# Sum of squares of x taken from its features instead of its rows, in the first stage of a two-layer hybrid block on one core

## What is computed

```python
def _rmsnorm(x, w=None):
    xf = x.astype(jnp.float32)
    y = xf * lax.rsqrt(jnp.mean(xf * xf, axis=-1, keepdims=True) + NORM_EPS)
    return y if w is None else y * w.astype(jnp.float32)

def _hybrid_layer(h, norm_w, w_in, ...):
    u = _rmsnorm(h, norm_w)
    proj = jnp.matmul(u, w_in.astype(jnp.float32))
    ...
    return jax.nn.sigmoid(gate_a) * y_a + jax.nn.sigmoid(gate_b) * y_b

# h = x;  h = h + hybrid_layer(h);  then rmsnorm and two more layers
```

## Time and profile before

| what | value |
|---|---|
| median of 3 runs (lowest, highest) | 2182.87 us (2181.63, 2183.14) |
| the profiled execution, its own time | 2180.54 us |
| its span in the trace | 2178.9 us |
| TensorE busy | 2151.7 us, 99% of the span |
| VectorE, ScalarE, GpSimd busy | 59%, 51%, 6% |
| mean DMA share, read from HBM | 58% of 16 engines, 389.94 MB |
| granted clock, mean | 0.998 |

### The profile page before, as it was taken

One profiled execution on the slowest core, in us unless ns is written; L12 is line 12 of the kernel. 1 busy time (PEld: TensorE's weight loads), 2 busy tenths in 40 slices (PEclk: granted clock), 3 DMA queues, 4 the chain that ended last, 5 costly groups with the idle time before them and its releaser, 6 DMA issues.

```text
span 2178.9 us, 32768 instructions
## 1 busy us (share of the span) xinstructions
PE 2151.7 (99%) x12468; PEld 1774.4 (81%) x12468; DVE 1279.1 (59%) x1505; ACT 1110.3 (51%) x1478; POOL 125.1 (6%) x204
## 2 busy tenths in 40 slices
PE   9999999999999999999999999999999999999998
PEld 7888888888888777787878888888888788888886
DVE  6455546454545758575765564466545845566466
ACT  6544545544444748374655554455444544445442
POOL 6000000000000100001010000000000110000001
PEclk9999999999999999999999999999999999999999
DMA  9766565565655544454546765745568566555654
GB/s 349 246 189 192 169 202 178 183 202 184 200 186 183 156 145 145 127 168 124 174 137 207 238 193 179 205 146 164 161 197 271 177 214 169 163 163 164 194 167 143
DMA packets 208610, 400.64 MB, mean 184 GB/s; under 512 B 13296, under 2 KB 30209, under 8 KB 208094
## 3 DMA queue, kind: packets, MB, share of 16 engines
q1 hardware_dynamic: 199824, 369.94, 53.8%
q0 software_dynamic: 6352, 20.49, 3.1%
q10 hardware_dynamic: 2304, 8.39, 1.1%
HBM read 389.94 MB, written 8.82 MB: 183 GB/s over the span
## 4 chain that ended last, share of the span: by engine, by line
PE 89%; ACT 3%; DVE 3%; issue 3%; DMA 1%; DVEq 0%; ACTq 0%; SPq 0%
PE stream_psum L611 27%; PE stream_psum L613 26%; PE stream_psum L612 26%; PE heads_psum L592 2%; ACT w_high L1049 1%; PE heads_psum L774 1%; DVE work L1631 1%; ACT work L1049 1%; DVE w_low L1468 1%; PE heads_psum L961 1%; PE heads_psum L923 1%; PE heads_psum L904 1%; DMA w_raw<-in_w_mem_kv 1%; PE heads_psum L793 1%; PE heads_psum L722 0%
## 5 line engine op out<-in xcount | busy, mean ns | idle before, releaser
L1468 DVE TENSOR_TENSOR w_low<-w_raw,w_high 128x1024 fp32r<-128x1024 f32 x688 | 831.1, 1225 | 636.2 <-ACT w_high L1049 634.9
L1049 ACT ACTIVATE w_high<-w_raw 128x1024 fp32r<-128x1024 f32 x688 | 712.8, 1058 | 455.3 <-PE stream_psum L613 386.4
L611 PE MATMUL stream_psum<-w_high,x_high 128*128 128x512 f32 x1856 | 741.9, 400 | 0.1
L613 PE MATMUL stream_psum<-w_high,x_low 128*128 128x512 f32 x1856 | 724.2, 390 | 0.9 <-issue 0.9
L612 PE MATMUL stream_psum<-w_low,x_high 128*128 128x512 f32 x1856 | 723.4, 390 | 0.0
L613 PEld LDWEIGHTS stream_psum<-w_high,x_low 128*128 128x128 f32 x1856 | 348.3, 188 | 75.6 <-issue 1.8
L611 PEld LDWEIGHTS stream_psum<-w_high,x_high 128*128 128x128 f32 x1856 | 348.7, 188 | 73.3 <-issue 2.5
L612 PEld LDWEIGHTS stream_psum<-w_low,x_high 128*128 128x128 f32 x1856 | 348.9, 188 | 69.1 <-issue 1.9
L611 PE MATMUL stream_psum<-w_high,y_high 128*128 128x512 f32 x896 | 353.3, 394 | 2.7 <-DVE y_low L1887 2.2
L613 PE MATMUL stream_psum<-w_high,y_low 128*128 128x512 f32 x896 | 349.7, 390 | 0.0
L612 PE MATMUL stream_psum<-w_low,y_high 128*128 128x512 f32 x896 | 349.5, 390 | 0.0
(11 more groups left out here) (295 smaller groups left out, 1214.9 us busy)
## 6 DMA issues: line engine op xcount, KB each, us to landing
w_raw<-in_w_in SPq DMA_DIRECT2D x528, 512.0 KB, 4.5
w_raw<-in_w_out SPq DMA_DIRECT2D x128, 512.0 KB, 5.0
w_raw<-in_w_mem_kv SPq DMA_DIRECT2D x32, 512.0 KB, 5.8
work<-rows_scratch POOLq DMA_DIRECT2D x8, 512.0 KB, 5.0
proj<-in_mem_t SPq DMA_DIRECT2D x8, 256.0 KB, 6.3
work<-in_x_t SPq DMA_DIRECT2D x4, 512.0 KB, 6.0
residual<-in_x SPq DMA_DIRECT2D x2, 1024.0 KB, 10.5
mkv_scratch<-proj POOLq DMA_DIRECT2D x4, 512.0 KB, 3.6
```

Source lines behind the costliest of these rows:

```text
L611: pe.matmul(acc, hi[:, k, sl(m)], w, start=first, stop=False)
L613: return pe.matmul(acc, lo[:, k, sl(m)], w, start=False, stop=final)
L1049: return act.activation(dst, src, func, **kw)
L1468: tt(WL[:, c % RING, :], RAW[:, c % RING, :], WH[:, c % RING, :].bitcast(F32), ALU.subtract).then_inc(lo_done, 1)
```

## The change

1. **x features** come in eight pieces of 256 KB (two 128-feature tiles each) instead of four of 512 KB, one behind each weight chunk of the second memory block. ScalarE and VectorE work on one piece a chunk, over all eight chunks, instead of two pieces a chunk over four.
2. **Sum of squares**: the two Squares of x rows with `accum_out` go. ScalarE squares the x features in `wk(0)` to `wk(3)` into `wk(4)` to `wk(7)` in two instructions of 2048 columns; GpSimd halves the 4096 columns four times with additions of 2048, 1024, 512 and 256 columns; TensorE multiplies the 256 that remain with a matrix of ones, in the side `gates` of `N_ML`; Ln and Exp read PSUM.
3. **Order**: on ScalarE the Squares now stand ahead of `narrow_high`, and both behind the second memory block's copy out of PSUM. Ln and Exp move into `gates`, whose steps on TensorE, ScalarE and VectorE are put off with longer gaps.
4. **x rows** (`RES`) come in four pieces of 512 KB in `N_GA` instead of two of 1 MB in the memory stage. `gated(0)` waits for them.

```diff
-        xt_in = [sem(f"x_features{c}_in") for c in range(4)]
+        xt_in = [sem(f"x_features{c}_in") for c in range(NCH)]
+        x_sums, x_ss = sem("x_square_sums"), sem("x_squares_summed")
...
-        X_AFTER = ((1, 4), (1, 6))
...
             def x_features(i):
-                sp.dma_start(wk(i, U).rearrange("p (c n) -> p c n", c=2), bass.AP(x_t.tensor, i * (4 * P * S), [[2 * S, P], [2 * P * S, 2], [1, 2 * S]])
-                             ).then_inc(xt_in[i], 16)
+                sp.dma_start(wk(i / 2, 2 * S), bass.AP(x_t.tensor, i * (2 * P * S), [[2 * S, P], [1, 2 * S]])).then_inc(xt_in[i], 16)
...
-                    if (half, c) in X_AFTER:
-                        m = X_AFTER.index((half, c))
-                        sp.dma_start(RES[:, m, :], x2[:, m, :]).then_inc(x_in[m], 16)
-                    if half == 1 and c < 4:
+                    if half == 1:
                         x_features(c)
...
-            group(N_GA, w_in, 0, IN1, [wide(C_GA + b * NBLK) for b in range(4)])
+            for b in range(4):
+                for c in range(NCH):
+                    put(N_GA, b * NCH + c, rows_in_chunk(w_in, C_GA + b * NBLK, IN1, c, [[1, NBLK]]))
+                    if b in (1, 2) and c % 4 == 0:
+                        m, half = b - 1, c // 4
+                        sp.dma_start(RES[:, m, sl(half, U)], x2[:, m, sl(half, U)]).then_inc(x_in[m], 16)
...
+                if b == 0:
+                    pool.wait_ge(norm_s, 2)
+                    for i, n in enumerate((2 * U, U, U // 2, U // 4)):
+                        if i:
+                            pool.wait_ge(x_sums, i)
+                        pool.tensor_tensor(wk(4, n), wk(4, n), wk(4 + n / U, n), ALU.add).then_inc(x_sums, 1)
...
-                yield from gap(9)
+                yield from gap(8)
+                pe.wait_ge(x_sums, 4)
+                for m in range(M):
+                    last = pe.matmul(H[:, 1, sl(m, 8)], wk(4, S)[:, sl(m)], ones[:, 0:8], start=True, stop=True)
+                last.then_inc(x_ss, 1)
+                yield from gap(12)
...
                 for c in range(NCH):
-                    act.wait_ge(xt_in[c // 2], 16)
+                    act.wait_ge(xt_in[c], 16)
                     for k in (2 * c, 2 * c + 1):
                         f(XH[:, k, :], wk(k / 4, S), ACT.Copy, scale=NC_[:, k:k + 1]).then_inc(x_hi, 1)
+                    yield from gap(2)
+                act.wait_ge(consts, N_CONSTS)
+                for i in range(2):
+                    f(wk(4 + 2 * i, D), wk(2 * i, D), ACT.Square).then_inc(norm_s, 1)
                     yield
                 narrow_high(0, GATE_W, GATE_RAW)
                 yield
-                for m in range(M):
-                    act.wait_ge(x_in[m], 16)
-                    f(wk(4, D), RES[:, m, :], ACT.Square, accum_out=ST[:, m:m + 1]).then_inc(norm_s, 1)
-                    act.wait_ge(norm_s, m + 1)
-                    yield from gap(2)
-                f(ST[:, 2:4], ST[:, 0:2], ACT.Ln, scale=1.0 / D, bias=eps_c).then_inc(norm_s, 1)
+
+            def gates():
+                yield from gap(10)
+                act.wait_ge(x_ss, 1)
+                f(ST[:, 2:4], H[:, 1, 0:16].rearrange("p (m n) -> p m n", m=M)[:, :, 0], ACT.Ln, scale=1.0 / D, bias=eps_c).then_inc(norm_s, 1)
                 act.wait_ge(norm_s, 3)
                 f(ST[:, 4:6], ST[:, 2:4], ACT.Exp, scale=-0.5).then_inc(norm_s, 1)
-
-            def gates():
+                act.wait_ge(norm_s, 4)
+                yield from gap(2)
...
@@ DVE x_prep @@
-                    yield
+                    yield from gap(2)
                 narrow_low(0, GATE_W, GATE_RAW)
...
@@ DVE gates @@
+                yield from gap(11)
...
@@ DVE gated @@
+                    if not base:
+                        dve.wait_ge(x_in[m], 32)
```

More of the change, by code:

```diff
@@ L1358, in _ @@
             small_block(0, 48, G_ACT, wk(11, S)[0:96, :])
-            act.wait_ge(norm_s, 4)
             mkv = [[(mkv_out[b], 16)] for b in range(2)]
```

## The result

| | before | with the change |
|---|---|---|
| median of 5 runs (lowest, highest) | 2183.14 us (2181.63, 2185.22) | 2193.54 us (2193.38, 2196.36) |
| the profiled execution (its span) | 2180.54 us (2178.9) | 2196.36 us (2194.7) |
| TensorE busy | 2151.7 us, 99% | 2156.3 us, 98% |
| granted clock, mean | 0.998 | 0.993 |

The ratio is 1.0051 (95% interval 1.0041 to 1.0062): slower by 0.5%, 10.4 us between the medians, where 11.8 were forecast. The two profiled executions lie at opposite ends of their runs, before's under its lowest of these five and the other at its highest, so their spans differ by more, 15.8 us. What belongs to the change has to be read stage by stage.

What follows compares the result with a forecast made beforehand. TensorE was taken as the bound, busy 2151.7 of 2178.9 us. Terms 10.0 - 0.24 + 1.7 + 0.35 = +11.8 us, on the median 2182.87, gave 2194.7 us, range 2189.5 to 2197.5.

Steps and rivals of the forecast that it cites:

- start of the small block: TensorE's small block after the memory stage, waiting for narrow_low, starts at 64.75 instead of 54.74: +10.0 us.
- the edge behind it, and the clock: From small block to N_ML: wait for ScalarE's PSUM copy gone, -0.24 us; half clock behind the gap, +1.7 us.
- product of ones and the rest: Two small matmuls added to TensorE's stream in N_ML: +0.35 us (bounds 0.2 and 0.6).
- sum for the stage: All terms added, 10.0 - 0.24 + 1.7 + 0.35: +11.8 us.
- Queue order: ScalarE runs block copy, two Squares, then narrow_high, so the small block waits; alone its start moves to 60.7, +5.95 us.
- Standstill: VectorE's narrow_low waits out GpSimd's 2048-column addition of 4.9 us, moving the small block's start from 60.7 to 64.75.
- rival 2: No standstill: narrow_low isn't held up by GpSimd's addition, small block at 60.7, sum +7.8, 2190.6 us; chance 0.12.
- The clock: TensorE's 10.6 us idle before the small block halves its clock for 3.4 us of work: +1.7 us (bounds 0, 3.4).
- rival 3: More than forecast: low clock lasts twice as long (+1.7), or the gates' chain stalls chunks; 2196 to 2199 us; chance 0.10.
- The product of ones: Two small matmuls in TensorE's N_ML stream, 0.36 us between their start and the stream's next: +0.35 us.
- The covers: Margins in gates (least 0.9 us), last feature piece and x rows in N_GA: no new TensorE wait, 0 us.

Runs made afterwards that it cites:

- run 1: The changed kernel with narrow_high put ahead of the two Squares on ScalarE, both still behind the block copy: 2186.93 us, ratio 1.0009.
- run 2: The changed kernel with GpSimd's additions made to wait for narrow_low too: 2191.34 us, ratio 1.0030.
- run 3: The changed kernel with GpSimd's additions cut into instructions of at most 512 columns: 2190.95 us, ratio 1.0033.
- run 5: The changed kernel with 48 unread identity matmuls on TensorE ahead of the small block, filling its gap: 2184.33 us, ratio 1.0004.
- run 8: Run 7 with the x rows back in the memory stage as two pieces of 1 MB, those in N_GA removed: 2192.35 us, ratio 1.0038.
- run 6: The changed kernel with narrow_high and narrow_low moved into the second memory block, behind the seventh piece of x features: 2184.97 us, ratio 1.0003.
- run 7: The changed kernel with both the early split of run 6 and the 512-column additions of run 3: 2188.70 us, ratio 1.0019.
- run 9: The changed kernel with Squares of 512 columns behind each feature piece, 512-column additions between GpSimd's stores, and run 6's early split: 2187.05 us, ratio 1.0013.
- run 10: The kernel before the change with 24 identity matmuls added between the memory stage and the small block: 2180.25 us, ratio 0.9984.
- run 11: The kernel before the change with 24 small matmuls of 32x8 added right behind the warm-up ones: 2174.52 us, ratio 0.9956.

## Why the prediction was right

The time, 2193.54, lies 1.2 us from the forecast 2194.7 and inside 2189.5 to 2197.5. Step by step, by the sum's own terms:

| term | forecast | measured | by |
|---|---|---|---|
| start of the small block | +10.0 | +9.8 | 64.55 less 54.74 |
| the edge behind it, and the clock | -0.24 + 1.7 | +2.5 | 71.04 - 64.55 less 58.71 - 54.74 |
| product of ones and the rest | +0.35 | +0.4 | what is left to 12.75 |
| sum for the stage | +11.8 | +12.75 | block copies |

- **Queue order**: right. The memory blocks' end, forecast at 54.15, lets the block copy start at 54.38, with 0.2 us of a later start in it. Run 1 leaves the split behind the block copy and still takes 9.1 us away: the two Squares ahead of it (3.6), the standstill that they bring with them (3.7), and with the shorter gap 1.5 of the clock. The 5.95 of the forecast is another thing, the whole delay of the start without the standstill; run 2, which is that case, starts the small block at 60.45, +5.7.
- **Standstill**: right, rival 2 is out. Run 2 takes 4.1 us away, and run 3 shows that its length follows that of the addition. I took 4.9 us for the addition of 2048 columns, from the slope between 512 and 1024; it took 4.50. The rows weren't of one kind: both are multiplications, and the one of 1024 columns reads a mask over and over (L502). An addition of 1024 columns in run 2 takes 2.38 us instead of the 2.482 of the earlier trace rows. The Trainium skill, page "GPSIMD Engine Reference", section "Elementwise — side-by-side cycle accounting", gives 4497 ns: the trace agrees, with 4496. The rule of the Trainium skill, page "SBUF — State Buffer", section "Who interferes with whom", which I had assumed over 2048 columns, holds here: `narrow_low` took 4.63 us.
- **The clock**: right in kind, and **the term that was mis-sized**. "Half of 3.4 us: +1.7" was taken from one recovery at the start. Here the half clock lasted through 5.9 us of work, and run 5 prices it at 2.7 us, 1.0 more than the term. That lies inside its bounds (0 and 3.4), nearer to rival 3's "twice as long" than to my value. One recovery was no measure of the next.
- **The product of ones**: 0.37 us to the stream's next start (83.82 to 84.19), as in the rows I took it from, but the next start comes 0.31 behind that instead of 0.23: 0.45 in all, where I counted 0.35.
- **The covers**: right. No new wait in `gates`, for the last piece of features, or in `N_GA`; the wait for `w_low` at 51 is gone, and run 8 shows what can make it.
- **The close agreement is partly luck.** From the median before, 2183.14 + 12.75 would be 2195.9. The 2.3 us between that and 2193.54 come from the scatter of the executions and from the delta stage, which one profile of each doesn't measure: before's was 2.6 us under its median, the other 2.8 over. The forecast had no term for the delta stage at all; its "issue" waits, the largest group of TensorE's waits in the profile before, were passed over as no wait for another engine.

What stays open: why one place of the delta stage's instructions is better than another, whether other counts do more, and what of the +2.5 us there is the change's own and what is scatter; runs 1 to 3 and 6 to 9 have between +0.2 and +3.1 there, from TensorE programs of the same length. No other counts than 24 and 48 were tried.

## What to carry to other kernels

Taking work off a busy engine is worth nothing if the new work stands ahead of something small that the bounding engine needs next: look at what the moved instructions are queued in front of, on each in-order queue, and put the small producer (`narrow_high`, `narrow_low`) first or well ahead. A VectorE instruction with two SBUF inputs waits for the end of a GpSimd addition that began before it (3.7 us here, of 4.50); cutting the GpSimd work into pieces shortens VectorE's waits but starves GpSimd (15.5 us for 10.5), so pick the side that has the slack. An idle gap on TensorE costs its length and some us at half clock behind it (2.7 behind 10.2 us, 1.5 behind 2.9), and kernels should be compared by stage, since a stage that the edit doesn't touch can move by 7 us.

## What the runs showed of the hardware

- **TensorE's dense small matmuls depend on what stands ahead of them in its program.** Adding 24 or 48 matmuls ahead of them (at 54 us or at 7 us, before or with the change) makes the time from 105 us to the last block copy 6 to 8 us shorter, and the "issue" waits there fall from 5.6 us to 0.5 and 1.3. The instruction queues move the same in both cases (q8 36 transfers, q14 6, from 700 to 1180 us before and in runs 10 and 11), so it isn't their number. Why is open; that the waits are late fetches of instructions is only a guess. They stood in the profile before: the largest group of TensorE's waits is this one.
- **The recorded clock reads 1.00 before its first recorded change.** In the profile before, the warm-up products from 1.7 us on (12, recorded as 24; minimum, median and maximum duration in ns) begin at half pace and the last ones run at full pace, under a granted clock of 1.00:

```profile
L993 PE MATMUL heads_psum<-ident x24: 275/421/582, 1.7 to 6.2; 128*128 128x128 f32 x24
```

In runs 5, 10 and 11 the last of them starts at 6.8 instead of 6.2, the idle time behind is 1.44 us or less instead of 2.19, and the clock is full from the first product on. Near such a start a pace is a better witness than the record.
- **How long TensorE works at half clock behind a gap doesn't follow the gap's length alone.** It is 3.4 us of work behind the 2.19 us at the start before, 2.8 us behind the 2.94 of run 1 and 5.9 us behind the 10.21 of the change.
- **The exclusion between VectorE and GpSimd is mutual**: seven additions of 512 columns and one of 256 take 10.45 us beside a VectorE that is nearly idle (run 3) and 15.47 beside its `w_low` (run 7).
